# Memory attention of the recurrent layers: scores and value products from high and low halves instead of plain float32

## The reference

```python
def mem_cross_attention(h, mem_n, wq, wkv, wo):
    q = (h @ wq).reshape(B, T, XA_HEADS, XA_HEAD_DIM)
    kv = (mem_n @ wkv).reshape(B, M, 2, XA_HEADS, XA_HEAD_DIM)
    k, v = kv[:, :, 0], kv[:, :, 1]
    s = jnp.einsum('bthd,bmhd->bhtm', q, k).astype(jnp.float32) * (XA_HEAD_DIM ** -0.5)
    p = jax.nn.softmax(s, axis=-1).astype(h.dtype)
    o = jnp.einsum('bhtm,bmhd->bthd', p, v).reshape(B, T, D_MODEL)
    return o @ wo
```

## Time and profile before

| what | us |
| --- | --- |
| median of 3 runs | 3250.34 (3249.3 to 3250.51) |
| the profiled execution | 3248.06 |
| its span in the profile | 3246.3 |
| TensorE busy | 3213.2 (99%) |
| VectorE busy | 1698.0 (52%) |
| ScalarE busy | 1166.0 (36%) |
| attention, first recurrent layer | about 1676 to 1757 |
| attention, second recurrent layer | about 2764 to 2845 |

### The profile page before, as it was taken

How to read it: one execution, slowest core, us unless ns; L and a number is a source line. 1 busy time by engine, 2 the same in 40 slices (tenths; PEclk the granted TensorE clock), 3 DMA queues, 4 the chain that set the end, 5 groups by cost and what they waited for, 6 DMA issues and landing times.

```text
span 3246.3 us, 39625 instructions
## 1 busy us (share of the span) xinstructions
PE 3213.2 (99%) x14786; PEld 2634.1 (81%) x14786; DVE 1698.0 (52%) x2490; ACT 1166.0 (36%) x1847; POOL 0.2 (0%) x4
## 2 busy tenths in 40 slices
PE   9999999999999999999999999999999999999998
PEld 7777778788888888888887888888888888788887
DVE  6564445564544554346655554345443675465443
ACT  5663555532222322233533322232222344332222
POOL 0000000000000000000000000000000000000000
PEclk9999999999999999999999999999999999999999
DMA  4333333232222222232321222222223223132222
GB/s 145 102 94 98 95 100 104 84 118 94 96 95 97 97 97 97 98 110 75 117 85 65 94 95 96 97 98 97 97 97 113 86 90 112 46 101 95 96 97 91
DMA packets 90696, 313.32 MB, mean 97 GB/s; under 512 B 10192, under 2 KB 12624, under 8 KB 90192
## 3 DMA queue, kind: packets, MB, share of 16 engines
q1 hardware_dynamic: 83376, 294.69, 27.2%
q10 hardware_dynamic: 7200, 16.97, 1.7%
HBM read 309.52 MB, written 2.10 MB: 96 GB/s over the span
## 4 chain that ended last, share of the span: by engine, by line
PE 96%; DVE 2%; ACT 1%; issue 1%; DMA 0%; DVEq 0%; ACTq 0%
PE ps L1087 30%; PE ps L1089 29%; PE ps L1088 29%; PE ps L1274 1%; PE ps L1358 1%; PE ps L1263 1%; PE ps L1163 1%; PE ps L1252 1%; PE ps L1306 0%; PE ps L1289 0%; PE ps L1371 0%; PE ps L1255 0%; PE ps L1310 0%; PE ps L1395 0%; PE ps L1300 0%
## 5 line engine op out<-in xcount | busy, mean ns | idle before, releaser
L1087 PE MATMUL ps<-x_hi,whi 128*128 128x512 f32 x2400 | 945.0, 394 | 0.0
L1089 PE MATMUL ps<-x_hi,wlo 128*128 128x512 f32 x2400 | 934.7, 389 | 0.0
L1088 PE MATMUL ps<-x_lo,whi 128*128 128x512 f32 x2400 | 934.0, 389 | 0.0
L1412 ACT ACTIVATE whi<-raw 128x1024 fp32r<-128x1024 f32 (+1 forms) x555 | 583.2, 1053 | 897.4 <-DMA raw<-in_weights 895.1
L1699 DVE TENSOR_TENSOR wlo<-raw,whi 128x1024 fp32r<-128x1024 f32 x553 | 675.3, 1223 | 429.9 <-ACT whi L1412 421.1
L1087 PEld LDWEIGHTS ps<-x_hi,whi 128*128 128x128 f32 x2400 | 450.7, 188 | 97.6 <-issue 3.9
L1089 PEld LDWEIGHTS ps<-x_hi,wlo 128*128 128x128 f32 x2400 | 450.5, 188 | 94.5
L1088 PEld LDWEIGHTS ps<-x_lo,whi 128*128 128x128 f32 x2400 | 450.8, 188 | 94.0 <-issue 2.4
L1087 PE MATMUL ps<-h_hi,whi 128*128 128x512 f32 (+1 forms) x902 | 346.4, 384 | 0.0
L1089 PE MATMUL ps<-h_hi,wlo 128*128 128x512 f32 (+1 forms) x902 | 346.2, 384 | 0.0
L1088 PE MATMUL ps<-h_lo,whi 128*128 128x512 f32 (+1 forms) x902 | 346.2, 384 | 0.0
(11 more groups left out here) (290 smaller groups left out, 3312.4 us busy)
## 6 DMA issues: line engine op xcount, KB each, us to landing
raw<-in_weights SPq DMA_DIRECT2D x553, 512.0 KB, 3.2
bias<-in_biasB ACTq DMA_DIRECT2D x16, 384.0 KB, 3.2
bias<-in_biasA ACTq DMA_DIRECT2D x16, 256.0 KB, 3.1
mem_raw<-in_mem ACTq DMA_DIRECT2D x3, 1024.0 KB, 7.0
x_res<-in_x SPq DMA_DIRECT2D x8, 256.0 KB, 6.2
x_res<-in_x ACTq DMA_DIRECT2D x8, 256.0 KB, 3.3
out_x<-x_res SPq DMA_DIRECT2D x16, 128.0 KB, 1.9
raw<-in_weights SPq DMA_DIRECT2D x2, 256.0 KB, 4.2
```

The lines of the kernel that those rows point to most:

```text
L1087: pe.matmul(out, hi, xhi, start=start, stop=False)
L1088: pe.matmul(out, hi, xlo, start=False, stop=False)
L1089: return pe.matmul(out, lo, xhi, start=False, stop=stop)
L1412: return act.activation(out, in_, ACT.Copy, scale=scale)
```

## The change

Scores and value products of kind "X" use `three`. For that each query, key and value row is split (step `split`, generalised by `halves`), and each tile's transposed probabilities are split as well (new step `ptlo` on VectorE, semaphore `ptl`). The low halves of queries, keys and values overwrite the full values. The key splits 0 to 3 stand behind the first four `w_out_2` columns; query 0, keys 4 and 5 and values 0 and 1 behind query column 1; query 1, keys 6 and 7 and values 2 and 3 behind query column 2; query 2, values 4 to 7 behind the first turn; each later query row behind the turn that follows its column. The step `ptlo` of a tile stands behind the next `score`, or ahead of the next `turn` where no score comes between.

```diff
+        def low_halves():
+            for a in turned:
+                if a["kind"] == "X":
+                    step("ptlo", **a)
+            turned.clear()
+
         def turn(a):
+            low_halves()
             pv()
             step("turn", **a)
+            turned.append(a)
...
             step("score", **a)
+            low_halves()
...
+        def split_row(name, c, need):
+            step("split", id=(name, l, c), src=(name, c), dst=(name, c), need=need)
+
...
+                if s.behind_turn is not None:
+                    s.behind_turn.append(lambda: split_row("XQ", c, [("evac", jq[c])]))
...
+        queries[0]()
+        queries[1]()
+        split_row("XQ", 0, [("evac", jq[0])])
+        split_row("XK", 4, [mixed_out])
+        split_row("XK", 5, [mixed_out])
+        split_row("XV", 0, [mixed_out, ("xev", (x_group[0], NM // P - 1))])
+        split_row("XV", 1, [mixed_out, ("xev", (x_group[1], NM // P - 1))])
+        queries[2]()
+        split_row("XQ", 1, [("evac", jq[1])])
...
-        attend([dict(kind="X", h=h, t=t, l=l, need=[("evac", jk[2 * h + 1])], queries=(jq, 2 * h + 1),
-                     need_v=[("xev", (x_group[2 * h], NM // P - 1))]) for h in range(NHEAD) for t in range(NT)],
-               queries[3:] + [start for start, _ in begun], places=(3, 7, 11, 15, 20, 28, 30, 32))
+        attend([dict(kind="X", h=h, t=t, l=l, need=[("olo", ("XK", l, 2 * h + 1)), ("olo", ("XQ", l, 2 * h + 1))],
+                     need_v=[("olo", ("XV", l, 2 * h + 1))]) for h in range(NHEAD) for t in range(NT)],
+               queries[3:] + [start for start, _ in begun], places=(3, 7, 11, 15, 20, 28, 30, 32),
+               behind=[lambda: split_row("XQ", 2, [("evac", jq[2])]),
+                       *[lambda c=c: split_row("XV", c, [("xev", (x_group[c], NM // P - 1))]) for c in (4, 5, 6, 7)]])
...
-                            mm = pe.matmul(sc, XQ[:, 2 * h + c, tt], XK[:, 2 * h + c, :],
-                                           start=(c == 0), stop=(c == 1))
+                            qh, ql = halves(("XQ", 2 * h + c))
+                            mm = three(sc, qh[:, tt], ql[:, tt], *halves(("XK", 2 * h + c)), c == 0, c == 1)
...
-                    free[turn_slot(a)] = ("pt", i)
+                    free[turn_slot(a)] = ("ptl" if a["kind"] == "X" else "pt", i)
...
-                    pe.wait_ge(*on("pt", i))
+                    pe.wait_ge(*on("ptl" if what == "X" else "pt", i))
...
-                            mm = pe.matmul(O, XV[:, 2 * h, c * P:(c + 1) * P], PT[:, c, :], start=(c == 0), stop=(c == 1))
+                            cc = slice(c * P, (c + 1) * P)
+                            mm = three(O, XVH[:, 2 * h, cc], XVL[:, 2 * h, cc], PTH[:, c, :], PTL[:, c, :], c == 0, c == 1)
...
+                elif kind == "ptlo":
+                    i, t = a["i"], a["t"]
+                    dve.wait_ge(*on("pt", i))
+                    dve.tensor_tensor(PTL[:, :, t * P:(t + 1) * P], turned_in(a)[:, 0:2 * P].rearrange("p (c q) -> p c q", c=2),
+                                      PTH[:, :, t * P:(t + 1) * P].bitcast(F32), ALU.subtract).then_inc(*sig("ptl", i))
...
-                    dve.tensor_tensor(MIXL[:, c, :], buf(a["src"]), MIXH[:, c, :].bitcast(F32), ALU.subtract)\
-                        .then_inc(*sig("olo", a["id"]))
+                    dve.tensor_tensor(lo, buf(a["src"]), hi.bitcast(F32), ALU.subtract).then_inc(*sig("olo", a["id"]))
```

More of the change, by code:

```diff
@@ L338, in build_schedule, with attend @@
     ntiles = 0
-    def attend(tiles, work, after_pv=None, places=None):
+    def attend(tiles, work, after_pv=None, places=None, behind=()):
         nonlocal ntiles
@@ L348, in attend @@
         due = []
-        s.behind_turn = []
+        s.behind_turn = list(behind)
         def pv():
@@ L720, in build_schedule @@
             step("refresh", n=norm, m=m, gain=f"xa_norm_2_{l}", need=("evac", j))
+            if m < 4:
+                split_row("XK", m, [("evac", jk[m])])
+        mixed_out = ("evac", j)
         s.norms.append(("rstd", norm))
@@ L914, in program @@
         XK = area("x_k", 0, [P, DC, NM])
+        XQL, XKL = area("x_q_lo", 8, [P, DC, T], F32R), area("x_k_lo", 0, [P, DC, NM], F32R)
+        XQH = area("x_q_hi", 94, [P, DC, T], F32R)
+        XKH = [area(f"x_k_hi_{kb}", kb, [P, 2, NM], F32R) for kb in (110, 112, 68, 92)]
         XV = area("x_v", 24, [P, DC, NM])
@@ L927, in buf, with halves @@
             return bufs[where[0]][:, where[1], :]
+        def halves(where):
+            name, c = where
+            if name == "XK":
+                return XKH[c // 2][:, c % 2, :], XKL[:, c, :]
+            hi, lo = {"MIX": (MIXH, MIXL), "XQ": (XQH, XQL), "XV": (XVH, XVL)}[name]
+            return hi[:, c, :], lo[:, c, :]
         def col(name, m=0):
@@ L1242, in _ @@
                             pe.wait_ge(*on(*key))
-                        if what == "X":
-                            jq, c = a["queries"]
-                            pe.wait_ge(*on("evac", jq[c]))
                     slots, sc = score_bank(a)
@@ L1309, in _ @@
                         for c in range(2):
-                            mm = pe.matmul(TR[:, T:2 * T], XV[:, 2 * h + 1, c * P:(c + 1) * P], PT[:, c, :],
-                                           start=(c == 0), stop=(c == 1))
+                            cc = slice(c * P, (c + 1) * P)
+                            mm = three(TR[:, T:2 * T], XVH[:, 2 * h + 1, cc], XVL[:, 2 * h + 1, cc], PTH[:, c, :], PTL[:, c, :],
+                                       c == 0, c == 1)
                         free["T1"] = ("olo", ("X", a["l"], 2 * h + 1))
@@ L1601, in _ @@
                         nk = NT
-                    copy(PT[:, 0:nk, t * P:(t + 1) * P],
+                    copy((PTH if a["kind"] == "X" else PT)[:, 0:nk, t * P:(t + 1) * P],
                          turned_in(a)[:, 0:nk * P].rearrange("p (c q) -> p c q", c=nk)).then_inc(*sig("pt", i))
@@ L1616, in _ @@
                         act.wait_ge(*on(*key))
-                    copy(MIXH[:, a["dst"][1], :], buf(a["src"])).then_inc(*sig("ohi", a["id"]))
+                    copy(halves(a["dst"])[0], buf(a["src"])).then_inc(*sig("ohi", a["id"]))
                 elif kind == "evac" and a["evac"] == "branch" and a["b"] == 2:
```

17 lines of the change are left out of this document (11 added, 6 removed).

## The result

The changed kernel takes 3277.06 us (median of 6 runs, 3276.25 to 3278.64), the kernel before 3250.19 (6 runs, 3248.43 to 3251.32) on the same chip: 26.9 us slower, ratio 1.0084, 95% interval 1.0072 to 1.0097. The forecast was 3268.9, in a range of 3255 to 3280. The direction and most of the waits came as worked out; nearly 10 us came from one of the rivals, the clock, on top of the forecast. The narrower range of the forecast alone, 3262 to 3275, was missed by 2 us.

What follows compares the result with a forecast made beforehand. TensorE was taken to bound the kernel; new waits of about 14.4 us less 5.1 of saved work gave 9.3 a layer, +18.6 in two, so the median 3250.34 becomes 3268.9 us. Range 3255 to 3280; this case's own 3262 to 3275.

Steps and rivals of the forecast that it cites:

- the clock: Rival: TensorE's clock falls after long new waits in the attentions; six falls at 2.5 us cost 15, giving 3284; 10%.
- What bounds it: Whole kernel: TensorE busy 99% of the span, 96% of the chain; VectorE and ScalarE count only through waits on it.
- The work of TensorE: Both attentions: cheaper score and value products save 5.1 us a layer, 10.1 in all.
- After column 2: Scores 0 to 2: score 0 waits for query 1's low half; +2.3 us a layer. E is the column's end.
- After column 3: First turn: score 4 waits 3.5 us for query 2's low half behind four value rows; +3.3 a layer.
- After column 4: Attention behind query column 4: waits hidden, only two cheaper scores count; -0.3 us a layer.
- After column 5: Head 0's product, turn 5 and score 8, which waits for query 5's low half; -0.3 us instead of -1.0.
- After column 6: Head 1's product waits for the low half of tile 7's probabilities, starting at E + 5.17; +1.7 us a layer.
- After column 7: Score 12 waits for query 7's low half, then VectorE paces tiles at 1.70 us; +3.4 us a layer.
- The sum: Both attentions: waits of about 14.4 less 5.1 of work, 9.3 us a layer, +18.6 in two.
- Outside the attentions: Time outside the two attentions moving by more than 1 us would mean something was missed.
- The w_out_2 stage: Output columns ahead of the attention, where keys 0 to 3 are split: costs nothing, at worst 0.5 us.

Runs made afterwards that it cites:

- f3_order: Changed kernel with query columns and splits moved earlier, columns placed before head products, and tile low halves reordered on VectorE; 3246.82 us, ratio 0.9991.
- e1_scores: Changed kernel with only scores from halves; value rows and transposed probabilities not split; 3264.61 us, ratio 1.0049.
- e4_fill: Changed kernel plus useless matmuls before scores 4 and 12 and the products of heads 1 and 2; 3266.35 us, ratio 1.0057.
- e3_values_later: Changed kernel with the splits of value rows 4 to 7 behind the third turn instead of the first; 3268.13 us, ratio 1.0058.
- e2_values: Changed kernel with only probabilities by values from halves; queries and keys not split; 3251.02 us, ratio 1.0006.
- f5_plain_order: Kernel before, plain float32, with only the column placing of f3_order; 3249.41 us, ratio 1.0001.
- f7_turn_fill: f3_order plus useless matmuls, 2 before turn 13 and 7 before turn 14; 3244.59 us, ratio 0.9984.
- f1_earlier: Changed kernel with four query columns ahead of the attention, query rows split one column later, value rows 4 to 7 with columns 5 and 6; 3254.43 us.
- f4_values_order: f3_order with only probabilities by values from halves, scores plain float32; 3250.06 us, ratio 0.9998.
- f6_five_inside: f3_order with three query columns ahead and five inside the attention instead of four ahead; 3249.2 us, ratio 0.9996.

## Why the prediction was right, and where it was not

- *What bounds it.* TensorE is still 95% of the chain, and the change acted through waits on it alone.
- *The work of TensorE.* Steps of 0.12 and 0.228 as forecast (scores 0 and 1 in the changed kernel: 10 steps from 1684.50 to 1685.69, 0.119 each). The saving of 10.1 us is the difference of TensorE's busy time between f3_order and before; that it fits to the tenth is luck, since both profiles have slow stretches, of about the same length. In the changed kernel the slow stretches hid it (3217.4).
- *After column 2.* Forecast wait 1.7 and column 3 at E + 5.50; measured 1.62, and 5.48.
- *After column 3.* Forecast: score 4 waits 3.5; measured 3.47. The order of VectorE's rows was read rightly. Column 4 came at 1699.83, E + 6.04 instead of 5.35: 0.6 of it is the clock.
- *After column 4.* Forecast -0.3, measured -0.3 (column 5 at E + 1.70).
- *After column 5.* Score 8 waited 0.41, forecast some 0.5.
- *After column 6.* Product of head 1 at E + 4.86, forecast 5.17; it waited 2.99, forecast 3.3. The term that was too large is VectorE's chain for a tile: 1.70 forecast, 1.56 measured (reductions at 1728.68 and 1730.24), because the low half of the transposed probabilities starts 0.07 behind the start of the negation and not the 0.19 of a full step.
- *After column 7.* Score 12 at E + 3.73, forecast 3.75. Product of head 2 at E + 9.65, forecast 9.3: that looks near, but with the clock held it is 8.91, again by the shorter chain (1.57), and the clock added 0.7. And e1_scores showed that ScalarE's part in score 12's wait is larger than I had it, so the right number had a reason that was partly wrong.
- *The sum.* 18.6 forecast, 17.2 measured with the clock held (e4_fill). That 3277.06 lies in the range of 3255 to 3280 is owed to the width of that range, which I had drawn without this cause in mind.
- *The missing term.* The clock was priced as a rival of 10%, as if it and the forecast excluded each other. It is a term of the same sum: 9.7 us by e4_fill, against the 15 that I gave it. I had put each of six falls at 2.5 us; in the first layer the three cost 2.7, 1.6 and 0.7. And the sentence that the profile before shows no case was false. I had read the granted clock in the attention and nowhere else; at the start I had inferred it from the steps of the first six matmuls. The profile of before gives 1.00 there:

```profile
0.00:6.40 6.40, 4.95 (x6) 1.85 (x6) 0.48 (x1) 2.03 (x3) 0.20 (x4) 1.00 0.69 207
```

Column and steps (0.79 us instead of 0.43) disagree, and which is right isn't settled; the 2.5 us a fall rested on it. The kernel before, in its mixers (windows as in the earlier trace rows):

```profile
1565.00:1568.00 3.00, 2.21 (x5) 1.82 (x6) 2.17 (x5) 0.63 (x1) 0.00 (x0) 0.60 0.00 0
2651.00:2654.00 3.00, 3.00 (x12) 2.61 (x11) 2.96 (x5) 0.42 (x1) 0.00 (x0) 0.51 0.03 10
```

and TensorE in order of time ahead of and in the first of these:

```profile
1562.73 1.14 PE L1358 MATMUL ps<-h_qt,h_q 128*128 128x128 f32 x8 [1.90 <-DVE h_qt L2056]
1565.79 0.77 PE L1087 MATMUL ps<-whi,mem_hi 128*128 128x512 f32 x1 [1.91 <-DVE x_k L1855]
1566.35 0.63 PE L1088 MATMUL ps<-wlo,mem_hi 128*128 128x512 f32 x1
1566.78 0.63 PE L1089 MATMUL ps<-whi,mem_lo_a 128*128 128x512 f32 x1
```

Two waits of 1.9 us with 1.1 of work between, and a 512-column step of 0.43 behind them. With this seen I would have held a fall behind waits of 3 us for likelier than not, and its price for a term of the forecast. The Trainium skill's rule that I cited ("TensorE: Matmul & The Clock Gate", section "Why this matters for your kernels"), that an idle gap between bursts, if long enough, returns the clock to half rate, fits the fall behind the single wait of 3.47 us (0.70 over the next 9 us). The falls of the kernel before stand behind shorter gaps: the two of 1.9 us shown, and in the second layer's mixer a single one of 1.91 us (matmuls at 2650.59).
- *Outside the attentions.* I had said that a move of over 1 us would mean something missed. The profiled span moved by 2.2 us there, 1.6 of it within the first 26 us. What I had missed is the clock once more, by chance: ahead of the first product of the program TensorE waited 2.16 us for a weight's low half (1.51 before), its six matmuls having ended earlier. The product itself starts only 0.05 us later than before (7.96 and 7.91), but slowly:

```profile
6.00:9.00 3.00, 1.04 (x3) 0.84 (x4) 2.41 (x4) 2.08 (x4) 0.00 (x0) 0.82 0.94 310
9.00:12.00 3.00, 3.00 (x10) 2.39 (x9) 1.75 (x3) 2.25 (x3) 0.00 (x0) 0.61 1.05 414
```

Nothing in the change touches that place, and the wait scatters from profile to profile (0.79 to 2.16 in the table above). The w_out_2 stage gave 0.1, as forecast.

## What to carry to other kernels

When a product is split into more and cheaper matmuls, look first for where its new halves stand behind an evacuation that the next matmul waits for; split each row one column later and put a tile's own subtraction behind what the next turn wants, and the loss of 27 us becomes a gain of 2.4, at the edge of the interval; with the last wait filled it is 5.3. Read the granted clock over the whole span, not only where the change is: each wait of a few us carries its own length and often the slow stretch behind it. Where such a wait can't be removed, a few matmuls that nobody reads can be worth their place.

## What the runs showed of the hardware that I had not expected

- Waits of 1.6 to 1.7 us standing by themselves (score 4 in e1_scores and e3_values_later) had no fall of the clock behind them in their profiles; those of 2.7 to 3.5 us mostly had, but not each time (3.00 in e3_values_later: 1.00; 2.80 at score 12 in the second layer of e1_scores: none). The same wait at the start of the program, behind the same six matmuls, had a fall behind it in the four profiles in which it took 1.88 to 2.16 us, and none in the nine in which it took 0.79 to 1.70. Close together, shorter ones had one too: 1.90 and 1.91 in the mixer before, 0.57 and 1.82 at the last turns of f3_order, 1.44 in e3_values_later 4 us behind another fall. Even equal waits differ. In the second layer's mixer every profile waits some 1.9 us; a fall follows at once in five (before, changed, e2_values, f5_plain_order, f7_turn_fill). In the other eight a wait of 2.8 us follows after 1.1 us of work; it has a fall behind it in three (f1_earlier, f4_values_order, f6_five_inside) and none in five. What makes it fall or not isn't settled by these runs.
- A fall costs nothing where TensorE would wait anyway. In the second layer's mixer of before the clock falls behind the first of two waits (0.51) and the second wait is 1.18 us; in f3_order it doesn't fall and the second wait is 2.80; the stretch between the attentions takes 963.6 and 963.8 us.
- A matmul on data that is not needed keeps the clock as one that is: 46 of them per layer in e4_fill, 9 in f7_turn_fill.
- One and the same program spreads over 6 us (f6_five_inside), more than many changes are worth, and the mean granted clock goes with it, 0.998 to 0.995. That the clock is all of it isn't shown: no fast run of that program was profiled.
